# Window attention: the inverse of the softmax denominators as exp(-ln) on ACT instead of four reciprocals on DVE

## The reference

```python
def gqa_softmax(q, k, v, mask, sink):
    s = jnp.einsum('bkgqd,bkjd->bkgqj', q, k, preferred_element_type=jnp.float32) * (q.shape[-1] ** -0.5)
    if mask is not None:
        s = jnp.where(mask, s, NEG)
    ...
        sk = sink.astype(jnp.float32)[None, :, :, None, None]
        m = jnp.maximum(s.max(axis=-1, keepdims=True), sk)
        e = jnp.exp(s - m)
        p = e / (e.sum(axis=-1, keepdims=True) + jnp.exp(sk - m))
    return jnp.einsum('bkgqj,bkjd->bkgqd', p.astype(v.dtype), v)
```

## Time and profile before

| | before |
|---|---|
| median of three runs | 3208.64 us |
| profiled execution, its own time | 3204.82 us |
| its span | 3202.8 us |
| TensorE busy | 3057.2 us, 95% |
| DVE busy | 1816.9 us, 57% |
| ACT busy | 1285.8 us, 40% |
| POOL busy | 540.7 us, 17% |
| mean granted clock of TensorE | 0.975 |

### The profile page before, as it was taken

One profiled execution on the slowest core, in us unless ns is written; L12 is line 12 of the kernel. 1 busy time (PEld: TensorE's weight loads), 2 busy tenths in 40 slices (PEclk: granted clock), 3 DMA queues, 4 the chain that ended last, 5 costly groups with the idle time before them and its releaser, 6 DMA issues.

```text
span 3202.8 us, 46649 instructions
## 1 busy us (share of the span) xinstructions
PE 3057.2 (95%) x19340; PEld 2680.9 (84%) x19340; DVE 1816.9 (57%) x2712; ACT 1285.8 (40%) x2197; POOL 540.7 (17%) x530
## 2 busy tenths in 40 slices
PE   7999999999999999999999988898999999999998
PEld 6987878789999999999999966556788878878887
DVE  7675545546666552545657667684554543355353
ACT  4464555433223363654323345332432332243231
POOL 0002222123112000003202313111210211122020
PEclk9899999999999999999999999999999999999999
DMA  3210000024554521013464541001232222222232
GB/s 107 73 48 34 1 1 1 35 88 137 178 184 136 181 82 60 1 61 126 134 215 145 166 146 44 36 1 46 73 101 90 91 87 99 96 79 93 90 100 82
DMA packets 79507, 284.33 MB, mean 89 GB/s; under 512 B 8480, under 2 KB 9248, under 8 KB 78528
## 3 DMA queue, kind: packets, MB, share of 16 engines
q1 hardware_dynamic: 79296, 281.35, 26.4%
HBM read 274.96 MB, written 6.36 MB: 88 GB/s over the span
## 4 chain that ended last, share of the span: by engine, by line
PE 83%; DVE 9%; DMA 3%; ACT 3%; issue 1%; POOL 0%; DVEq 0%; SPq 0%; ACTq 0%; POOLq 0%
PE psum L345 57%; DMA araw<-d_ada 3%; PE psum L1193 2%; PE psum L839 2%; PE psum L1783 2%; PE psum L1214 2%; PE psum L1980 1%; PE psum L1225 1%; DVE wlo L302 1%; DVE araw L426 1%; PE psum L1222 1%; DVE rdn L2674 1%; PE psum L1962 1%; PE psum L2598 1%; PE psum L1953 1%
## 5 line engine op out<-in xcount | busy, mean ns | idle before, releaser
L302 DVE TENSOR_TENSOR wlo<-wraw,whi 128x1024 fp32r<-128x1024 f32 (+2 forms) x398 | 498.9, 1279 | 638.2 <-ACT whi L295 629.4
L295 ACT CAST whi<-wraw 128x1024 fp32r<-128x1024 f32 (+2 forms) x398 | 395.8, 1022 | 509.4 <-PE psum L345 477.5
L426 DVE CUSTOM_DVE_ANT_0 araw<-araw,cond 128x1024 f32<-128x1024 f32 x112 | 137.4, 1236 | 80.6 <-DMA araw<-d_ada 80.5
L345 PE MATMUL psum<-f0xh,whi 128*128 128x264 f32 x704 | 144.3, 287 | 6.4 <-DVE f0xl L540 3.9
L345 PE MATMUL psum<-f1xh,whi 128*128 128x264 f32 x704 | 143.8, 286 | 5.4 <-DVE f1xl L540 3.9
L345 PE MATMUL psum<-f0xh,wlo 128*128 128x264 f32 x704 | 143.9, 286 | 0.0
L345 PE MATMUL psum<-f3xh,whi 128*128 128x512 f32 x352 | 139.9, 397 | 4.2 <-DVE f3xl L536 4.2
L345 PE MATMUL psum<-f2xh,whi 128*128 128x512 f32 x352 | 139.8, 397 | 4.2 <-DVE f2xl L536 4.2
L345 PE MATMUL psum<-f1xh,wlo 128*128 128x264 f32 x704 | 143.6, 286 | 0.0
L345 PE MATMUL psum<-f0xl,whi 128*128 128x264 f32 x704 | 143.4, 285 | 0.0
L345 PE MATMUL psum<-f1xl,whi 128*128 128x264 f32 x704 | 142.9, 284 | 0.0
(11 more groups left out here) (510 smaller groups left out, 8671.8 us busy)
## 6 DMA issues: line engine op xcount, KB each, us to landing
wraw<-d_w SPq DMA_DIRECT2D x357, 512.0 KB, 3.4
araw<-d_ada SPq DMA_DIRECT2D x112, 512.0 KB, 3.3
wraw<-d_w SPq DMA_DIRECT2D x32, 384.0 KB, 3.2
hn<-d_h SPq DMA_DIRECT2D x4, 528.0 KB, 7.4
hres<-d_h SPq DMA_DIRECT2D x1, 2112.0 KB, 8.2
spill<-hres SPq DMA_DIRECT2D x1, 2112.0 KB, 7.4
hres<-spill SPq DMA_DIRECT2D x1, 2112.0 KB, 8.6
cond<-d_cond SPq DMA_DIRECT2D x2, 1024.0 KB, 5.0
```

Source lines behind the costliest of these rows:

```text
L295: e.copy(whi[0:rows, n % NH, 0:kt * cols], wraw[0:rows, n % NR, 0:kt * cols]).then_inc(*w_hi.up(n))
L302: e.tensor_tensor(wlo[0:rows, n % NH, 0:kt * cols], wraw[0:rows, n % NR, 0:kt * cols], whi[0:rows, n % NH, 0:kt * cols].bitcast(F32), ALU. ...
L345: ins = e.matmul(psum[0:bw, b0 + nb * len(sl) + si, 0:ln], l_ if z == 2 else h_, (xp.lo if z == 1 else xp.hi)[:, k, o:o + ln], start=k == ...
L426: e.tensor_tensor_reduce(out=w, in0=w, in1=self.c[:, col, :], scale=1.0, scalar=0.0, op0=ALU.mult, op1=ALU.add, accum_out=ada[:, ly, blk, ...
```

## The change

Two steps of "end" go to ACT. At q=0 ACT takes the logarithm of all 512 denominators of a group at once, on 64 partitions, from PSUM into rdn (it waits for the group's last product, t_v, and for rdn's earlier reader, t_o). At q=1 it takes in place the exponential of minus that. The four reciprocals on DVE are gone; DVE's two multiplications move from q=3 to q=2 and wait for ACT's second step (t_r). The scaling of the residual block and ACT's copy stay at q=3.

```diff
@@ -2542,7 +2542,7 @@
         t_k = sig("t_k", wk("key"))
         t_p = sig("t_p", wk("key"))
         t_v = sig("t_v", [(g, q) for g, q in wk("val")])
-        t_r = sig("t_r", wk("end"))
+        t_r = sig("t_r", [(g, q) for g, q in wk("end") if q < 2])
         t_o = sig("t_o", [(g, p) for g, q in wk("end") if q == 3 for p in range(2)])
         t_oh = more(s_oh, [(g,) for g, q in wk("end") if q == 3])
         t_ol = more(o_lo, [(g,) for g, q in wk("end") if q == 3])
@@ -2632,6 +2632,15 @@
                     if n >= NP:
                         e.wait_ge(*t_v.at(*wk("key")[n - NP]))
                     e.activation(Pw[:, n % NP, :], psum[:, 4 + n % 2, :], ACT.Exp, scale=0.125).then_inc(*t_p.up(g, q))
+                elif s == "end" and q == 0:
+
+                    e.wait_ge(*t_v.at(g, NQ[g] - 1))
+                    if g >= 2:
+                        e.wait_ge(*t_o.at(g - 2, 1))
+                    e.activation(rdn[:, i, :], psum[64:128, 6 + i, :], ACT.Ln).then_inc(*t_r.up(g, 0))
+                elif s == "end" and q == 1:
+                    e.wait_ge(*t_r.at(g, 0))
+                    e.activation(rdn[:, i, :], rdn[:, i, :], ACT.Exp, scale=-1.0).then_inc(*t_r.up(g, 1))
                 elif s == "end" and q == 3:
                     cs_ = slice(128 * qb, 128 * qb + 128)
                     e.wait_ge(*t_o.at(g, 1))
@@ -2667,13 +2676,8 @@
                         e.tensor_scalar(dg[:, i, j, :], ident, nmr[:, i, j:j + 1].bitcast(F32), None, ALU.mult).then_inc(*t_dg.up(g, j))
                 elif s == "end":
                     b = 6 + g % 2
-                    if q == 0:
-                        e.wait_ge(*t_v.at(g, NQ[g] - 1))
-                        if g >= 2:
-                            e.wait_ge(*t_o.at(g - 2, 1))
-                    e.reciprocal(rdn[:, i, 128 * q:128 * q + 128], psum[64:128, b, 128 * q:128 * q + 128]).then_inc(*t_r.up(g, q))
-                    if q == 3:
-                        e.wait_ge(*t_r.at(g, 3))
+                    if q == 2:
+                        e.wait_ge(*t_r.at(g, 1))
                         if g >= 2:
                             e.wait_ge(*t_ol.at(g - 2))
                         for p in range(2):
@@ -2681,6 +2685,7 @@
                                             psum[0:64, b, :].rearrange("p (h x) -> p h x", h=4)[:, p::2, :],
                                             rdn[:, i, :].rearrange("p (h x) -> p h x", h=4)[:, p::2, :],
                                             ALU.mult).then_inc(*t_o.up(g, p))
+                    elif q == 3:
 
                         if 1 <= g <= 8:
                             if g == 1:
```

## The result

| | before | changed |
|---|---|---|
| median of four runs | 3208.93 us (3201.45 to 3210.72) | 3175.14 us (3173.43 to 3182.89) |
| profiled execution | 3204.82 us | 3173.93 us |
| its span | 3202.8 us | 3172.1 us |
| the stage: from group 1's first key product to the output projection's first product | 187.19 us | 156.31 us |

The ratio is 0.9901, with a 95% interval of 0.989 to 0.9913: 28 to 35 us faster. The prediction was 3179 us.

A forecast was written before the change was run, and what follows sets the result against it. TensorE was taken to bound the kernel, held up by late exponentials. Gains of 17.0 us (stalls), 9.1 (slow matmuls) and 2.0 (tail) sum to 28.1 us, giving 3179 us; range 3172 to 3191.

The forecast's parts named there:

- The bound and the mechanism: Attention stage: TensorE bounds; it waits for Pw's exponential, queued on ACT behind the previous group's copy, which waits for DVE.
- The stalls: TensorE's waits for Pw in the attention stage: 18.6 us fall to 1.6, a gain of 17.0 us.
- The slow matmuls: Matmuls after stalls run at the lower clock level; gain 9.1 us if the clock stays up.
- six of eight gaps: Groups of five tiles: late next exponentials in six cases put down to slow matmuls after TensorE idled over 2 us.
- a gap of 0.2 us is harmless: Attention stage: remaining 0.2 us gaps would be followed by no slow matmul, so the clock stays up.
- The tail: After the last group: logarithm and exponential, 1.4 us, replace four reciprocals of 3.39 us; gain 2.0 us.
- The added activations: ACT, per group: logarithm 0.69 us and exponential 0.63 us, 21 us in all, hidden in idle time at no cost.
- (A): Attention stage: stalls go but the clock still drops, leaving some slow spells; gain 17 to 21 us, about 3187; chance 0.16.
- (B): ACT becomes late elsewhere: 0.5 to 1 us TensorE wait per group, 8 to 16 us given back, 3187 to 3195; chance 0.10.
- (C): Hardly any gain, within 9 us: multiplications wait for ACT instead, or the chain returns through another queue; chance 0.05.
- (D): Slower: logarithm and exponential need different function tables, two switches per group; 19 us slower, some 3226 us; chance 0.03.

The follow-up runs named there:

- the doubled operations: Changed kernel with logarithm and exponential each taken twice, once into a scratch tile: stage 157.38 us, ratio to before 0.9909.
- the kernel with switches: Changed kernel with a one-column sigmoid in front of each logarithm, forcing function table loads: stage 214.92 us, ratio to before 1.0066.
- the kernel with the dial: Changed kernel with 1 to 4 more ACT exponentials before the late Pw in groups of five tiles: stage 168.46 us, ratio to before 0.9951.

## Why the prediction was right

**The bound and the mechanism** held. The end of group g-1 was a wait in ACT's queue ahead of an exponential that TensorE wanted. Moving the copy alone removes it, in the stage that was profiled.

**The stalls**, 18.6 us and 1.6 left: no gap of 0.2 us showed, but the 1.6 us are there. Groups of five tiles take 11.73 and 10.71 us in the changed kernel and 11.46 and 10.58 with copy later and projection early, 4x0.27+4x0.13 = 1.6 us. I had called them gaps; in the trace they stand as longer rows. The four products in the middle of group 13, in the changed kernel and in the one of before with the copy later:

```profile
2144.55 2.24 PE L2598 MATMUL psum<-Pw,vw 128*128 128x512 f32 x4
...
2147.78 1.97 PE L2598 MATMUL psum<-Pw,vw 128*128 128x512 f32 x4
```


**The slow matmuls**, 9.1 us predicted, are the mis-sized term. With 30.88 us in the stage, less 17.0 of stalls and 2.15 of tail, 11.7 us remain. Some 1.4 of that is 0.17 us behind each of the eight gaps, slow or not, as the dialled gaps show; the prediction had no term for it. That leaves some 10 us of slow matmuls. Against the second profile of before the same sum gives 180.84-156.31-17.1-2.15 = 5.3 us, and some 4 us of slow matmuls. So what I took from one profile as a property of the stalls differs from one execution to the next; the gain in the stage is 24.5 to 30.9 us, depending on the execution of before. The forecast of 28.1 lies between them, partly by luck, and the reason given for six of eight gaps, over 2 us of idle time, was incomplete. That a gap of 0.2 us is harmless was right; beyond that the length is no guide, since 24 gaps of up to 1.94 us were harmless and four of 1.88 us were not.

**The tail**, 2.0 us: 2.15 measured. **The added activations** at 0.69 and 0.63 us: 0.59 and 0.62, and hidden, even twice. **Rivals:** (A) did not occur, since no gap was left; (B) fell with the doubled operations; (C) fell with the gain itself, and the multiplications wait for ACT in the last two groups alone; (D) is real as a mechanism, but the changed kernel has no load in the stage. The Trainium skill (ScalarE: Activation LUTs, "Table sets: the hidden batching unit") names a set with exp and ln. The changed kernel agrees: no load in the stage. The Trainium skill (the same page, "What ACT_TABLE_LOAD costs") also gives about 2.7 us for a switch with the drain. In the kernel with switches a load took 1.283 us, and the idle time in front of all 48 loads is at most 3.5+0.3+0.3 us, 3.2 of it a single wait ahead of the last group's sigmoid, so no such drain shows on ACT here.

In the medians the gain is 3208.93-3175.14 = 33.8 us, 5.7 more than the forecast of 28.1; between the two profiled executions it is 30.9, and when the changed kernel was measured again it was 26.3. The 3179 was counted from 3207, below the median of before. So the absolute number was met within a scatter that is larger than the miss.

## What to carry to other kernels

Look for in-order queues in which an instruction that is wanted now stands behind one that waits for another engine; moving the waiting one back by one place can be worth nearly as much as removing the work that it waits for (here a stage of 158.67 against 156.31 us). Before moving work between engines ask who wants the result and when: with the reciprocals on DVE the stage was 2.4 us longer than the changed kernel's with the result wanted late, and 16 us with the result wanted early. A logarithm and exponential pair on ACT is a good inverse only while a function table that holds both stays loaded.

## What the runs showed of the hardware

- A reciprocal on DVE takes 956 ns for 64x128; the logarithm and the exponential on ACT take 594 and 618 ns for 64x512. For 512 denominators that is 3.4 us against 1.2 us.
- With a sigmoid among them, the logarithm and the exponential no longer share a table load in this program: 48 loads of 1283 ns for 16 sigmoids.
- Behind gaps of 2.1 to 2.7 us TensorE ran at the lower level of its clock (granted 0.94, 0.97 and 0.95 over the stage in three executions, behind six, two and five of eight long gaps), or did not (1.00 with gaps of 2.46 and 2.60 us); the same program differed by 6.35 us in this stage between two executions. Of the shorter gaps, 24 of up to 1.94 us in four kernels were followed by nothing slow, and all four of 1.88 us in the kernel with table switches were.
- Each gap costs 0.17 us beyond the length that the profile gives it: group 13 took 14.23 us in the kernel with the dial, with a gap of 2.60, and 11.46 with copy later and projection early, without any. Overlap of matmuls that has to start again would explain it; since the ends of matmuls are modelled, the runs don't show this.
